# The order of the merge's branches and of the weight splits in a two-layer decoder step

## The reference

```python
z = h @ w_in                         # q, k, v, gates of all branches
y_ml = head_rmsnorm(hm, ml_g) * jax.nn.sigmoid(mo)
y_gla = head_rmsnorm(og, gla_g) * jax.nn.silu(go)
br = jnp.stack([y_ml, y_gla, y_pool], axis=2)
proj = jnp.einsum('btnc,ncd->btnd', br, w_branch)
gate = jax.nn.sigmoid(gates.reshape(B, T, N_BRANCH, D_MODEL))
mixed = jnp.sum(gate * proj, axis=2) @ w_out
```

## Time and profile before

| | |
|---|---|
| time, median of 3 runs | 2287.2 us |
| profiled execution, its own time | 2290.17 us |
| its span | 2288.5 us |
| busy: PE / DVE / ACT / POOL | 94% / 59% / 39% / 9% |
| merge, layer 0 | about 475 to 558 us of the span |
| expert passes | about 1617 to 2250 us of the span |

### The profile page before, as it was taken

The page is one execution under the profiler, slowest core; times in us unless marked ns, Lnnn a source line. Parts: engine busy times, 40 slices in busy tenths (PEclk is TensorE's granted clock), DMA queues, the critical chain, the costliest instruction groups (busy, mean ns, idle before and its releaser), DMA issues.

```text
span 2288.5 us, 38882 instructions
## 1 busy us (share of the span) xinstructions
PE 2148.6 (94%) x15567; PEld 1991.1 (87%) x15567; DVE 1358.5 (59%) x2015; ACT 899.1 (39%) x1253; POOL 216.0 (9%) x328
## 2 busy tenths in 40 slices
PE   7999999989999999999999999897799999999994
PEld 7998889889999999999988889897678888888883
DVE  5563346477555553345634464766478877877876
ACT  4312221543432322233122216333455555555554
POOL 0002220221000000000031202201100000000011
PEclk9999998999999999999999999998799999999996
DMA  4222234355522222222232344532577767777785
GB/s 177 76 91 90 74 121 139 131 164 187 214 91 90 90 92 92 95 91 74 95 99 73 116 144 144 159 125 88 195 230 235 250 228 238 230 245 235 236 269 161
DMA packets 103391, 341.77 MB, mean 149 GB/s; under 512 B 13592, under 2 KB 17720, under 8 KB 103000
## 3 DMA queue, kind: packets, MB, share of 16 engines
q1 hardware_dynamic: 85416, 278.46, 37.8%
q0 software_dynamic: 17856, 61.59, 7.9%
HBM read 294.28 MB, written 46.17 MB: 149 GB/s over the span
## 4 chain that ended last, share of the span: by engine, by line
PE 72%; DVE 9%; issue 7%; ACT 7%; DMA 4%; POOL 1%; ACTq 0%; DVEq 0%; SPq 0%; POOLq 0%
PE ps L1799 46%; PE ps L1793 9%; PE ps L2130 6%; PE ps L2144 4%; ACT w_hi L729 4%; DMA raw<-slabs 3%; DVE w_lo L1110 3%; PE ps L2132 3%; PE ps L2148 3%; DVE gt L1479 1%; DVE mixed L1484 1%; DVE gs L1432 1%; POOL br_lo L638 1%; DVE gsum L1694 0%; POOL token_slots L681 0%
## 5 line engine op out<-in xcount | busy, mean ns | idle before, releaser
L1110 DVE TENSOR_TENSOR w_lo<-raw,w_hi 128x1024 fp32r<-128x1024 f32 x488 | 601.3, 1232 | 367.1 <-ACT w_hi L729 362.6
L729 ACT ACTIVATE w_hi<-raw 128x1024 fp32r<-128x1024 f32 x488 | 510.7, 1052 | 454.6 <-PE ps L1799 396.0
L1799 PE MATMUL ps<-h_hi,w_hi 128*128 128x260 f32 x2544 | 535.7, 292 | 24.0 <-DVE h_lo L1119 13.8
L1799 PE MATMUL ps<-h_lo,w_hi 128*128 128x260 f32 x2544 | 519.3, 286 | 0.0
L1799 PE MATMUL ps<-h_hi,w_lo 128*128 128x260 f32 x2544 | 519.1, 286 | 0.0
L1799 PEld LDWEIGHTS ps<-h_hi,w_hi 128*128 128x128 f32 x2544 | 402.0, 192 | 49.7 <-issue 28.9
L1799 PEld LDWEIGHTS ps<-h_lo,w_hi 128*128 128x128 f32 x2544 | 400.3, 192 | 0.0
L1799 PEld LDWEIGHTS ps<-h_hi,w_lo 128*128 128x128 f32 x2544 | 399.4, 192 | 0.0
L2130 PE MATMUL ps<-hg,w_hi 128*128 128x320 f32 x1408 | 370.6, 346 | 3.0 <-DVE hg L1560 1.8
L2132 PE MATMUL ps<-hg,w_lo 128*128 128x160 f32 x1408 | 334.6, 238 | 0.0
L2130 PEld LDWEIGHTS ps<-hg,w_hi 128*128 128x128 f32 x1408 | 266.0, 189 | 13.9 <-DVE w_lo L1110 4.5
(11 more groups left out here) (369 smaller groups left out, 2728.3 us busy)
## 6 DMA issues: line engine op xcount, KB each, us to landing
raw<-slabs SPq DMA_DIRECT2D x489, 512.0 KB, 4.0
gates_kept<-sq SPq DMA_DIRECT2D x64, 260.0 KB, 2.1
gs<-gates_kept POOLq DMA_DIRECT2D x64, 260.0 KB, 3.8
token_slots<-zeros POOLq DMA_DIRECT2D x1, 9600.0 KB, 34.7
rows_in<-token_slots POOLq DMA_DIRECT2D x9, 512.0 KB, 5.3
Cs<-ml_C POOLq DMA_DIRECT2D x8, 512.0 KB, 4.8
C_s<-Cs POOLq DMA_DIRECT2D x8, 512.0 KB, 3.5
token_slots<-yt POOLq DMA_DIRECT2D x8, 512.0 KB, 3.3
```

What stands on the lines that cost most here:

```text
L729: nc.scalar.activation(w_hi[:, n % SPL], raw[:, place(n)], ACT.Copy).then_inc(hi_ready, 1)
L1110: tt_op(w_lo[:, n % SPL], raw[:, place(n)], w_hi[:, n % SPL].bitcast(F32), ALU.subtract).then_inc(lo_ready, 1)
L1799: ins = mm(out[:, hf], wgt_part[:, slot, tile], in_part[:, kk, HALF * hf:HALF * (hf + 1)], start=first and not ends and in_part is in_hi, ...
```

## The change

1. Merge: the three slabs of a pair of tiles are now pooling, mLSTM, GLA, with both outputs of a slab from one branch. SyncE's load builds the mLSTM and GLA slabs out of two neighbouring slabs (two runs of 2 KB for each partition, 8 slabs per layer; `slab_source`, not shown), and the gate columns are loaded in the matching order.
2. Low parts: POOL's 8 are removed, DVE makes all 12 (`branch_lo`), and DVE rounds the four pooling tiles to `br_hi`. The split of the third merge slab and the reading out of the first (`branch_outs(l, 0, 0)`) move into `gates`. TensorE waits for a branch's low parts just ahead of that branch's first slab.
3. Fills: a slab's split and reading out stand ahead of a wait instead of behind it, in GLA (ACT and DVE), in head norm and gates (ACT). In mLSTM it is the other way round: the exponentials (ACT) and `wcol` (DVE) stand ahead of the slab.
4. Routing: one `split_lo` leaves the chain of router logits.
5. Expert pass: a pass's first sigmoid table load stands at the loop's head; the splits around a pass's end take another order on DVE and ACT; the addition of the rest rows (`add_rest`) moves from the end of a pass into the first step of the next, and the main rows are stored on a semaphore of their own.

```diff
-            def branch_rest(t, nth):
...
-            pool.wait_ge(y_added, j * 2 + 3)
+            pool.wait_ge(y_main, j + 2)
             pool.dma_start(slots[bass.ds(j * CAP, P)], yt[:, 0]).then_inc(y_stored, 16)
+            pool.wait_ge(y_added, j + 2)
             pool.dma_start(slots[bass.ds(j * CAP + P, REST)], yt[0:REST, 1]).then_inc(y_stored, 16)
...
             nc.scalar.activation(dec[:], dec[:], ACT.Ln, bias=1.0).then_inc(g.sem, 1)
+            fill(2)
...
-                fill(2)
...
-                fill(2)
+                fill(4)
...
                 nc.scalar.activation(mixed[:, t:t + 2], mixed[:, t:t + 2], ACT.Exp,
                                      scale=-0.5).then_inc(hn_rs, 1)
+                if t == 2:
+                    fill(2)
...
         def gates(l):
             for k in range(AHEAD):
                 gate_sigmoid(l, k)
-            fill(2)
-            for j in (8, 9, 10, 11, 0, 1, 2, 3, 4, 5, 6, 7):
-                if j < 8:
-                    act.wait_ge(gated, 8 * l + j + 1)
+            for j in range(2 * H):
+                if j < LAST_FILL:
+                    fill(2)
+                elif j == LAST_FILL:
+                    filled(l)
+                    split_hi(l * LAYER1 + S_BRANCH + 2)
+                act.wait_ge(gated, 8 * l + j + 1)
                 nc.scalar.activation(br_hi[:, j], br[:, j], ACT.Copy).then_inc(br_hi_ready, 1)
-                if j < 8:
-                    gate_sigmoid(l, j + AHEAD)
-                    fill(2)
+                gate_sigmoid(l, j + AHEAD)
...
-                split_hi(nb + S_BRANCH + s + 2)
+                if s > 0:
+                    split_hi(nb + S_BRANCH + s + 2)
...
+            last = FE_TILES - 1
             for f in range(FE_TILES):
-                if f > 0:
+                if f > 1:
                     split_hi(s0 + gate_slab(f) + 2, j)
-                else:
+                elif f == 0:
+                    nc.scalar.activation(msig[0:1, 0:1], eps[0:1], ACT.Sigmoid).then_inc(table_loaded, 1)
                     split_hi(s0 + gate_slab(f) + 3, j)
-                    nc.scalar.activation(msig[0:1, 0:1], eps[0:1], ACT.Sigmoid).then_inc(table_loaded, 1)
                 act.wait_ge(m_sum, f0 + (f + 1))
                 if f == 0:
                     act.wait_ge(table_loaded, j + 1)
                 nc.scalar.activation(msig[:], gsum[:], ACT.Sigmoid).then_inc(m_sig, 1)
-                if f > 0:
+                if f > 1:
                     split_hi(s0 + gate_slab(f) + 3, j)
-                if f > 0:
+                if f == 0:
+                    split_hi(s0 + down_slab(0), j)
+                elif f < last:
                     split_hi(s0 + down_slab(f - 1) + 2, j)
-                if f == FE_TILES - 1:
-                    gathered_hi(j + 1, 1)
                 act.wait_ge(m_act, f0 + (f + 1))
                 nc.scalar.activation(ma_parts[:, f % 2, 0:CAP], ma[:, f % 2], ACT.Copy).then_inc(m_hi, 1)
-            split_hi(s0 + down_slab(FE_TILES - 1) + 2, j)
+                if f == 0:
+                    split_hi(s0 + down_slab(0) + 1, j)
+            split_hi(s0 + down_slab(last - 1) + 2, j)
+            gathered_hi(j + 1, 1)
             gathered_hi(j + 1, 0)
+            split_hi(s0 + down_slab(last) + 2, j)
             split_hi(s0 + 2, j + 1)
             act.wait_ge(slab_done, j * S_JOB + (s0 + S_JOB))
             act.wait_ge(y_stored, j * 32 + 16)
+            act.wait_ge(y_added, j + 1)
...
             inc(tt_op(la[:], la[:], dec[:], ALU.subtract))
+            fill(2)
...
-                fill(2)
                 at("exps")
                 inc(nc.vector.tensor_copy(wcol[:], wgt[:, :, NP_TOK - 1]))
+                fill(2)
...
             for k in range(AHEAD):
                 gate_scale(l, k)
+            dve.wait_ge(hn_ssq, 8 * (l + 1))
+            for t in range(2 * H, 3 * H):
+                nc.vector.tensor_copy(br_hi[:, t], br[:, t]).then_inc(br_hi_ready, 1)
+            for t in range(2 * H, 3 * H):
+                branch_lo(l, t)
             fill(2)
...
+                if k > 0:
+                    branch_lo(l, k - 1)
+                if k < LAST_FILL:
+                    fill(2)
+                elif k == LAST_FILL:
+                    fill(2 * N_FILL - fills[0])
+                    split_lo(l * LAYER1 + S_BRANCH + 2)
+                elif k == LAST_FILL + 1:
+                    branch_outs(l, 0, 0)
+            for i in range(2):
+                gate_scale(l, 2 * H + AHEAD + i)
+            branch_lo(l, 2 * H - 1)
+
+        def branch_lo(l, t):
+
+            dve.wait_ge(br_hi_ready, 12 * l + (t + H) % (3 * H) + 1)
+            tt_op(br_lo[:, t], br[:, t], br_hi[:, t].bitcast(F32), ALU.subtract).then_inc(br_lo_ready, 1)
+
+        def branch_outs(l, mp, s):
+
+            n, ob = l * LAYER1 + S_BRANCH + 3 * mp + s, l * O_LAYER1
+            for i in range(2):
+                if i == 0:
+                    dve.wait_ge(first_out_done, 12 * l + 3 * mp + s + 1)
+                else:
+                    out_done(n)
+                k = 2 * H + 6 * mp + 2 * s + i
+                o = ob + branch_out(k)
+                at = gate_back(l, k)[0]
+                dve.wait_ge(gate_sig, N_GATES * l + k + 1)
+                steps = 16 * l + 4 * mp + 2 * (s - 1) + i
+                if s > 0 and steps > 0:
+                    dve.wait_ge(mix_steps, steps)
+                to = gt[:] if s else mixed[:, 2 * mp + i]
+                tt_op(halves(to), out_ps(o), halves(gs[:, at]), ALU.mult).then_inc(
+                    emptied[o % 2], 1)
+                if s > 0:
+                    dve.wait_ge(*evac(o))
+                    dve.wait_ge(*evac(ob + branch_out(2 * H + 6 * mp + i)))
+                    tt_op(mixed[:, 2 * mp + i], mixed[:, 2 * mp + i], gt[:], ALU.add).then_inc(
+                        mix_steps, 1)
+                if mp + s > 0:
+                    gate_scale(l, k + AHEAD)
...
+                for s in range(3):
                     n = nb + S_BRANCH + 3 * mp + s
...
+                    if n > nb + S_BRANCH:
+                        split_lo(n + 2)
+                        branch_outs(l, mp, s)
...
-            split_lo(MOE0 + 2)
...
+            last = FE_TILES - 1
             for f in range(FE_TILES):
-                split_lo(s0 + gate_slab(f) + (2 if f else 3), j)
-
+                if f > 1:
+                    split_lo(s0 + gate_slab(f) + 2, j)
                 dve.wait_ge(slab_done, j * S_JOB + (s0 + gate_slab(f) + 1))
                 b = 2 * (f % 2)
                 nc.vector.tensor_reduce(gsum[:], addends(b), AX.X, ALU.add).then_inc(m_sum, 1)
+                if f == 0:
+                    split_lo(s0 + 2, j)
+                    split_lo(s0 + gate_slab(f) + 3, j)
                 dve.wait_ge(m_sig, f0 + (f + 1))
                 tt_op(ma[:, f % 2], gsum[:], msig[:], ALU.mult).then_inc(m_gate, 1)
-                if f > 0:
+                if f == 1:
+                    split_lo(s0 + down_slab(0) + 2, j)
+                elif 1 < f < last:
                     split_lo(s0 + gate_slab(f) + 3, j)
                 dve.wait_ge(slab_done, j * S_JOB + (s0 + gate_slab(f) + 2))
                 nc.vector.tensor_reduce(usum[:], addends(b + 1), AX.X, ALU.add).then_inc(m_up, 1)
                 dve.wait_ge(m_up, f0 + (f + 1))
                 tt_op(ma[:, f % 2], ma[:, f % 2], usum[:], ALU.mult).then_inc(m_act, 1)
-                if f > 0:
+                if f == last:
+                    split_lo(s0 + gate_slab(f) + 3, j)
+                elif f == 0:
+                    split_lo(s0 + down_slab(0), j)
+                elif f > 1:
                     split_lo(s0 + down_slab(f - 1) + 2, j)
-                if f == FE_TILES - 1:
-                    gathered_lo(j + 1, 1)
                 lo_of_act(f, f0)
-            split_lo(s0 + down_slab(FE_TILES - 1) + 2, j)
+                if f == 0:
+                    add_rest(j + 1)
+                    split_lo(s0 + down_slab(0) + 1, j)
+            split_lo(s0 + down_slab(last - 1) + 2, j)
+            gathered_lo(j + 1, 1)
             gathered_lo(j + 1, 0)
+            split_lo(s0 + down_slab(last) + 2, j)
             dve.wait_ge(slab_done, j * S_JOB + (s0 + S_JOB))
             dve.wait_ge(y_stored, j * 32 + 16)
-            nc.vector.tensor_copy(yt[:, 0].rearrange("p (a d) -> p a d", a=2), ps[:, 4:6]).then_inc(y_added, 1)
-            split_lo(s0 + 2, j + 1)
-            dve.wait_ge(y_copied, j + 1)
+            nc.vector.tensor_copy(yt[:, 0].rearrange("p (a d) -> p a d", a=2), ps[:, 4:6]).then_inc(y_main, 1)
+
+        def add_rest(n):
+
+            dve.wait_ge(y_copied, n)
             rest_rows = yt[0:REST, 1].rearrange("p (a d) -> p a d", a=2)
             tt_op(rest_rows, rest_rows, ps[REST:2 * REST, 6:8], ALU.add).then_inc(y_added, 1)
...
-                for s, outs in enumerate(((0, 1), (0, 1), (2, 2))):
+                for s, branch in enumerate((2, 0, 1)):
```

(41 more changed lines are left out.)

43 lines of the change are left out of this document (6 added, 37 removed).

## The result

The changed kernel takes 2246.9 us (median; 2246.4 to 2247.4), against 2287.5 before: a ratio of 0.9824, 95% interval 0.9809 to 0.984, or 40.6 us less. The forecast was 2252 with a range of 2224 to 2270. Its profiled execution took 2246.4 with a span of 2244.7; beside the 2290.2 of the profiled execution before that is 43.8 less.

A forecast was written before the change was run, and what follows sets the result against it. TensorE, busy in 94% of the span, was held by waits and the half clock behind some. Terms 2.7 + 5.4 + 12.8 + 0.8 - 0.9 + 12.6 + 1.8 = 35.2 took the profiled 2290.2 to 2255, median about 2252; range 2224 to 2270.

The forecast's parts named there:

- GLA, 2.7: GLA: DVE's split and reading of `q` move ahead of eight scans, removing a 1.33 us wait twice; gain 2.7.
- mLSTM, 5.4: mLSTM: exponentials ahead of the split start about 2.5 us earlier, removing four `wcol` waits of 1.3 to 1.4; gain 5.4.
- Gates and merge, 12.8: Gates and merge: gate-column wait goes, POOL's wait moves, merge splits stay 6.79 us apart but start earlier; 6.4 per layer.
- the chain: Gates: ACT, DVE and gate 13's transfer until TensorE's GLA slab near 487.7; boundary: third slab's transfer, then ACT and DVE work.
- Routing, 0.8: Routing: a split of 1.2 us leaves the router-logit chain; gain 0.8, since the copy behind it waits for a transpose.
- Pass boundaries, 12.6 and 1.8, less 0.9: Expert passes: 1.8 at each of seven boundaries, 1.8 at the eighth pass's end, less a new 0.9 wait in the first pass.
- the forecast's own signs of being wrong: A wait for the slab's transfer at the boundary, half clock staying at 2100, or merge splits no longer 6.8 apart.
- Five new waits: Pass boundary: 0.6 and 0.5 us at fourth slab and first down slab, then 0.9, 1.5 and 0.65; sum 4.2.
- the waits would vanish altogether: Rival, pass boundaries: third slab lands early and hand-overs overlap better; 28 us more gained, 2224; chance 0.14.
- No half clock stayed at the boundary: Against the rival that the clock still falls there after the 1.5 wait: about 12 us back, 2264; chance 0.2 shared with gates' chain.
- A table load has no stop behind it: Forecast counted the bare 1.28 us; rival, a similar stop follows, returning 1.3 at each of seven boundaries: 2261, chance 0.05.
- The slower case: Rival, pass boundary: third slab's load lands 11 us after issue instead of 4.3, 47 us lost: 2299; chance 0.04.

The follow-up runs named there:

- the edit undone: The changed kernel with the fills of GLA and mLSTM in their old places, head norm's slab left as changed: 2253.2 us, 6.3 more than the changed kernel.
- the passes alone: The kernel before with only the routing and expert-pass parts (4 and 5) of the change: 2270.2 us, 18.5 less than before, ratio 0.992.
- the later reading out: The changed kernel with the first merge slab read out behind the last GLA tile instead of ahead of it: 2245.5 us, 1.4 less than the changed kernel.
- the two splits: The changed kernel with the splits of a pass's seventh and eighth slab one place earlier on ACT and DVE: 2233.2 us, 13.7 less than the changed kernel.
- the run with one more load: The changed kernel with one more table load ahead of the sigmoid at each pass's head: 2259.6 us, 12.7 more than the changed kernel.

## Why the prediction was right

**GLA, 2.7.** The waits went and came back with the edit undone, both to the tenth. By the table the stage gave 1.5 in layer 0 and nothing in layer 1, where a half-clock stretch of 3.4 now lies at 1114 to 1117, worth 1.7.

**mLSTM, 5.4.** The wait of 5.4 was right; the stage gave 4.7 and 3.2. Of the 4.7 the clock gave about 1.6: before, a half-clock stretch reached 3.3 us into the stage (188 to 195), and after it none does.

**Gates and merge, 12.8.** 7.2 and 7.1, with the steps as forecast; 1.7 of each is the half clock at the gate column, which went. DVE's timeline in the changed kernel:

```profile
466.66 0.76 DVE L1465 SCALAR_TENSOR_TENSOR br<-br,vec,mixed 128x520 f32<-128x520 f32 x1
...
470.02 1.30 DVE L1508 TENSOR_TENSOR mixed<-ps,gs 128x520 f32<-128x520 f32 x2
...
474.60 0.69 DVE L1448 TENSOR_TENSOR gs<-gs,rs 128x520 f32<-128x520 f32 x1
476.76 0.70 DVE L1448 TENSOR_TENSOR gs<-gs,rs 128x520 f32<-128x520 f32 x1 [1.47 <-DMA gs<-gates_kept]
...
479.11 1.23 DVE L1126 TENSOR_TENSOR w_lo<-raw,w_hi 128x1024 fp32r<-128x1024 f32 x1 [1.04 <-ACT w_hi L736]
480.26 0.69 DVE L1508 TENSOR_TENSOR gt<-ps,gs 128x520 f32<-128x520 f32 x1
...
485.90 1.22 DVE L1126 TENSOR_TENSOR w_lo<-raw,w_hi 128x1024 fp32r<-128x1024 f32 x1 [1.65 <-ACT w_hi L736]
...
492.86 1.22 DVE L1126 TENSOR_TENSOR w_lo<-raw,w_hi 128x1024 fp32r<-128x1024 f32 x1 [1.66 <-ACT w_hi L736]
```

The pooling slab is read out at 470.0 (TensorE had waited 1.2), a gate is scaled at 474.6, and then DVE waits 1.47 for gate 13's transfer, as the chain had it; the split follows at 479.1 and the GLA slab at 481.1. The forecast had 487.7, on a time axis on which GLA and mLSTM had gained nothing; less the 6.2 gained there it is 481.5. The splits then stand 6.79 and 6.96 apart, about the pace of the earlier trace rows. DVE's added low parts cost nothing in the fills, as forecast (TensorE is busy 29.7 of 30.0 us from 440 to 470), and the slabs in two pieces landed in time: ACT waits for no transfer in the merge.

**Routing, 0.8.** Too small: 4.2, from 89.2 to 85.0 between the marks. Half clock lay from 1581 to 1591 before, for 10.2 us, and for 3.4 after. Three runs with the same edit at this place (the passes alone, the later reading out, the two splits) kept a stretch of 10.2 and took 87.1, 87.4 and 87.5. So with the clock alike the edit is worth 1.6 to 2.0, twice the forecast, and the rest of the 4.2 came with the shorter stretch. Seven of the ten traces with the edit have it and none of the three without, so whether the edit or chance shortened it is open; the forecast had no term for it.

**Pass boundaries, 12.6 and 1.8, less 0.9.** 13.5 forecast, 15.9 by the table. The end wait went, no stretch at half clock stayed, and the third slab's transfer came up as the next limit, as the chain had it. ACT's wait for it is by the letter one of the forecast's own signs of being wrong; but its chain has this transfer on the path too, and no line of TensorE waits for a transfer in the passes. ACT's and DVE's timelines at the boundary of the earlier trace rows:

```profile
2053.33 1.06 ACT L736 ACTIVATE w_hi<-raw 128x1024 fp32r<-128x1024 f32 x1 [1.72 <-DMA raw<-slabs]
...
2055.31 1.28 ACT L1042 ACT_TABLE_LOAD   x1
...
2056.71 1.04 ACT L736 ACTIVATE w_hi<-raw 128x1024 fp32r<-128x1024 f32 x1
```

```profile
2057.78 1.22 DVE L1126 TENSOR_TENSOR w_lo<-raw,w_hi 128x1024 fp32r<-128x1024 f32 x1 [1.56 <-ACT w_hi L736]
...
2061.48 1.21 DVE L1768 TENSOR_TENSOR yt<-yt,ps 32x1024 f32<-32x1024 f32 x1
...
2065.70 1.23 DVE L1126 TENSOR_TENSOR w_lo<-raw,w_hi 128x1024 fp32r<-128x1024 f32 x1 [0.62 <-ACT w_hi L736]
...
2069.05 1.23 DVE L1126 TENSOR_TENSOR w_lo<-raw,w_hi 128x1024 fp32r<-128x1024 f32 x1 [0.56 <-ACT w_hi L736]
```

The third slab's split waits for `raw<-slabs`; copy, one table load and the fourth slab's split follow without a pause; DVE waits 1.56 for that split, and behind the addition (2061.48) it waits for ACT before each of two splits. Five new waits were forecast, 0.6, 0.5, 0.9, 1.5 and 0.65, in sum 4.2. TensorE's rows show 0.37, 0.14, 0.81, 1.12 and 0.32, in sum 2.8; the three longest:

```profile
2059.06 0.41 PE L2184 MATMUL ps<-hg,w_hi 128*128 128x320 f32 x1 [0.37 <-DVE w_lo L1126]
...
2066.98 0.42 PE L2184 MATMUL ps<-hg,w_hi 128*128 128x320 f32 x1 [0.81 <-DVE w_lo L1126]
...
2070.40 0.49 PE L2198 MATMUL ps<-w_hi,ma_parts 128*128 128x512 f32 x1 [1.12 <-DVE w_lo L1126]
```

So the forecast set the new waits 1.4 too long, and what the clock gives back too high. Two of the seven intervals between result copies had no half clock before, 77.3 and 77.6 us (the table with the table load); after, the seven take 76.6 in the mean. That is 0.8 per boundary without the clock, for the forecast's 4.1 - 4.2 = -0.1, and it leaves 1.2 of the 2.0 gained to the clock, for the forecast's 1.7 (estimates, from two intervals; why the shorter waits show as 0.8 and not as 4.1 - 2.8 = 1.3 is open). That 1.8 came near 2.0 is in part luck: the two parts are off in opposite directions. Nor did the half clock stand behind the 2.2 us wait each time: at five boundaries it did, at two it began at the end wait (1696.8 and 1853.8).

The mechanism of the boundary is the one that the two runs on it show: a table load on ACT lengthens it, and fewer hand-overs shorten it.

**The rivals.** That the waits would vanish altogether failed, though two splits' order alone closes over half of the distance (2233, from 2247 towards 2224). No half clock stayed at the boundary; that it was near is seen in the run with one more load, where it came back four times. A table load has no stop behind it, as forecast. The slower case did not come: the transfer's landing was on the path, at its usual length (a median of 4.3 in the passes).

The sum of 35.2 stands against 40.6 of the medians and 43.8 of the two profiles. By stage the traces gave 9.4 for 8.1 (GLA and mLSTM), 14.3 for 12.8, 4.2 for 0.8 and 15.9 for 13.5. No step failed; routing is the term that was furthest off, and more than half of its surplus is the clock of the two executions.
